# The triangular inverse of a recurrent scan: its loop rotated by half a pass on TensorE

## The reference, cut to what matters

```python
def step(s, inp):
    w, kk, a, k, v, r = inp
    sa = jnp.einsum('dbhij,dbhj->dbhi', s, kk)
    s = s * w[..., None, :] - sa[..., :, None] * (kk * a)[..., None, :] + v[..., :, None] * k[..., None, :]
    return s, jnp.einsum('dbhij,dbhj->dbhi', s, r)
return lax.scan(step, s0, scan_in)
```

## Time and profile before

| | us |
|---|---|
| median of 3 runs (lowest, highest) | 2728.82 (2727.08, 2732.63) |
| the profiled execution | 2732.08 |
| its span, first to last instruction | 2730.3 |
| PE busy in the span | 2520.4 (92%) |
| one pass of the inverse's loop | about 4.4 |
| the 8 steps of the scan | about 1511 to 1880 of the span |

### The profile page before, as it was taken

The page is one execution under the profiler, slowest core; times in us unless marked ns, Lnnn a source line. Parts: engine busy times, 40 slices in busy tenths (PEclk is TensorE's granted clock), DMA queues, the critical chain, the costliest instruction groups (busy, mean ns, idle before and its releaser), DMA issues.

```text
span 2730.3 us, 51612 instructions
## 1 busy us (share of the span) xinstructions
PE 2520.4 (92%) x22056; PEld 1724.2 (63%) x22056; DVE 1276.9 (47%) x2865; ACT 598.8 (22%) x1349; POOL 506.0 (19%) x418
## 2 busy tenths in 40 slices
PE   8999999999999999998999899999998977787887
PEld 6688785476886843444678888888866533333333
DVE  2873310037731101156448434444228667777765
ACT  1243000013330000115333444332002111111111
POOL 0000000000000000000012444430003455544452
PEclk9999999999999999999999999999999999888989
DMA  5333333344234435323352101003348999999997
GB/s 188 147 120 124 136 150 150 129 178 155 93 124 154 153 147 218 156 81 145 148 199 64 33 18 34 18 11 125 124 170 315 411 421 421 421 421 422 422 421 309
DMA packets 91234, 523.81 MB, mean 192 GB/s; under 512 B 39728, under 2 KB 39728, under 8 KB 43440
## 3 DMA queue, kind: packets, MB, share of 16 engines
q0 software_dynamic: 39360, 277.51, 24.9%
q1 hardware_dynamic: 51696, 243.80, 24.0%
HBM read 511.85 MB, written 9.44 MB: 191 GB/s over the span
## 4 chain that ended last, share of the span: by engine, by line
PE 68%; DVE 11%; DMA 10%; issue 3%; PEld 3%; ACT 2%; DVEq 2%; POOL 1%; ACTq 0%; PEldq 0%; SPq 0%; POOLq 0%
PE psum L523 34%; PE psum L1597 25%; DMA mem<-weights,mem 9%; DVE mem L2921 4%; PE psum L2052 4%; PEld psum L1597 3%; PE psum L765 2%; DVE mem L2428 1%; PE psum L539 1%; PE psum L2024 1%; POOL mem L3065 1%; DVEq L2549 1%; PE psum L1607 1%; DVE mem L2879 0%; DMA mem<-weights 0%
## 5 line engine op out<-in xcount | busy, mean ns | idle before, releaser
L1597 PE MATMUL psum<-mem 64*64 64x64 f32 (+5 forms) x16032 | 919.3, 258 | 51.2 <-issue 22.1
L523 PE MATMUL psum<-mem 128*128 128x256 f32 (+10 forms) x4248 | 954.9, 397 | 7.5 <-DVE mem L1079 3.3
L1597 PEld LDWEIGHTS psum<-mem 64*64 64x64 f32 (+2 forms) x16032 | 725.3, 144 | 244.5 <-issue 160.3
L523 PEld LDWEIGHTS psum<-mem 128*128 128x128 f32 (+5 forms) x4248 | 692.1, 182 | 262.6 <-issue 168.2
L2052 PE MATMUL psum<-mem 128*128 128x512 f32 x1024 | 501.5, 648 | 119.3 <-ACT mem L2392 119.3
L2052 PEld LDWEIGHTS psum<-mem 128*128 128x128 f32 x1024 | 207.5, 207 | 406.9 <-issue 244.4
L3065 POOL DMA_INDIRECT mem<-weights,mem x256 | 317.6, 1241 | 531.0 <-PE psum L2052 265.7
L2921 DVE CUSTOM_DVE_ANT_0 mem<-mem 128x1024 f32<-128x1024 f32 x256 | 307.4, 1224 | 140.0 <-DMA mem<-weights,mem 133.6
L2428 DVE TENSOR_TENSOR mem<-psum,mem 128x512 f32<-128x512 f32 (+1 forms) x193 | 131.1, 683 | 270.0 <-PE psum L1597 244.8
L2971 POOL TENSOR_TENSOR mem<-mem 128x512 f32<-128x512 f32 (+2 forms) x132 | 168.9, 1296 | 207.2 <-DVEq L2674 154.1
L2428 DVE TENSOR_TENSOR mem<-mem 128x512 f32<-128x512 f32 (+7 forms) x211 | 137.8, 661 | 89.2 <-ACTq L2160 67.5
(11 more groups left out here) (244 smaller groups left out, 1322.8 us busy)
## 6 DMA issues: line engine op xcount, KB each, us to landing
mem<-weights SPq DMA_DIRECT2D x100, 2048.0 KB, 7.3
rates_dram<-mem POOLq DMA_DIRECT2D x16, 512.0 KB, 4.9
mem<-rates_dram SPq DMA_DIRECT2D x32, 256.0 KB, 4.7
mem<-weights SPq DMA_DIRECT2D x7, 1024.0 KB, 6.0
mem<-weights SPq DMA_DIRECT2D x2, 2176.0 KB, 8.0
mem<-weights,mem POOLq DMA_INDIRECT x256, 26.4
mem<-weights SPq DMA_DIRECT2D x2, 1536.0 KB, 8.4
mem<-weights SPq DMA_DIRECT2D x2, 1152.0 KB, 8.8
```

The lines of the kernel that those rows point to most:

```text
L523: ins = pe.matmul(out, lhsT, rhs, start=start, stop=stop, skip_group_check=skip)
L1597: ins = pe.matmul(out, lhsT, rhs, start=start, stop=stop, skip_group_check=skip)
```

## The change

`inverse` is cut into `lefts(j)` and `updates(j)`. The left products of the first level in the loop are issued ahead of the opening of the four banks, the loop makes four passes of updates and then the next level's left products, and the last updates stand behind it. What is computed, and its order on PE, stays as it was.

```diff
         def inverse(h, left):
-            products = [[act_ring.open(pe, "held") for _ in range(2)] for _ in range(2)]
-            with pe.Fori(0, LEVELS - 1) as j:
+
+            def lefts(j):
                 for d in range(2):
                     pe.wait_ge(inverse_ready.sem, j * 2 + ((2 * LEVELS - 2) * h + d + 1))
...
                     last.then_inc(left_full.sem, 1)
+
+            def updates(j):
                 for d in range(2):
                     pe.wait_ge(left_ready.sem, j * 2 + ((2 * LEVELS - 2) * h + d + 1))
...
                     two.then_inc(inverseT_full.sem, 1)
+
+            lefts(0)
+            products = [[act_ring.open(pe, "held") for _ in range(2)] for _ in range(2)]
+            with pe.Fori(0, LEVELS - 2) as j:
+                updates(j)
+                lefts(j + 1)
+            updates(LEVELS - 2)
```

## The result

The changed kernel takes 2740.52 us (median of 12 runs, 2735.27 to 2746.24), the kernel before 2731.91 us beside it (12 runs, 2726.84 to 2737.07). The ratio is 1.0036, 95% interval 1.0027 to 1.0045: slower by 7.4 to 12.3 us, where I had forecast 3.1 us, "within". The profiled execution took 2739.89 us with a span of 2738.1, which is 7.8 us more than the span before.

The account below looks back on a forecast made before the run. PE was taken as the bound, with new code in steps 4 to 7 paced by its own loading. -4.4 - 0.4 + 0 + 5.3 + 2.6 = +3.1 us on 2728.8 gave 2731.9 us, range 2723 to 2739.

Parts of the forecast that it names:

- The opening: Ahead of the loop in steps 0 to 3: four PE waits for ACT's bank copies shrink to 0.15 us each, -4.4 us.
- The code: Doubled calls around the loop: 12 more instruction packets, +5.3 us in steps 4 to 7 and +2.6 in steps 0 to 3.
- Full pace: New code in steps 4 to 7 runs at its loading pace, 3.8 us a packet: +1.3 us per step, +5.3 taken.
- The first rival: Doubled code: packets come early enough, so the code term is 0; 2724.0 us, chance 0.18.
- The branch and the passes: At the loop: 40 branches back become 32, -0.4 us; moving the branch ahead of the updates changes remaining passes by 0.
- The sum: Whole kernel: the terms make +3.1 us on 2728.8, so 2731.9 us, "within".
- Code costs nothing: Doubled code: packets come early enough, leaving -4.8 us, so 2724.0 us; chance 0.18.
- Updates behind the loop run dry: Behind the loop: each of eight exits stalls 1.6 us for a packet, +12.8 us, so 2736.8 us; chance 0.16.
- Another collision: Packets against loads of the rates: one collision more 2737.4 us, chance 0.08; one less 2726.4 us, chance 0.05.
- The wait does not go: At the opening: the wait becomes one for direction 1's mask or `left_ready`, losing -4.4; 2736.3 us, chance 0.04.
- Shorter passes: In the loop: the branch is hidden wholly and ACT's chain moves up, -4.1 us more; 2727.8 us, chance 0.07.
- The signs I had named: In the scan: 138 packets, issue waits up 5 to 10 us, 0.5 to 1.5 us gaps behind exits, passes at 4.4 us.

Follow-up runs that it names:

- e7: e6 with the wait for the product banks moved into the loop, between left products and updates, as in e1; 2725.92 us, ratio 0.9970 to the kernel before.
- e2: The changed kernel with the product banks opened ahead of the first left products again; 2739.96 us, ratio 1.0028 to the kernel before.
- e13: The changed kernel again with one comment more and no instruction changed; 2739.47 us, ratio 1.0027 to the kernel before.
- e8: The changed kernel with the loads of the rates and step 7's weight load held back as in e6; 2728.29 us, ratio 0.9983 to before.
- e15: e8 with the product banks opened ahead of the first left products, leaving only the doubled code of the change; 2732.64 us, ratio 1.0003 to before.
- e1: The kernel before with the wait for the product banks moved into the loop, between left products and updates; 2738.66 us, ratio 1.0017 to before.
- e10: e7 with 128 semaphore increments on PE ahead of the scan, half an instruction packet; 2743.55 us, ratio 1.0042 to the kernel before.
- e3: The changed kernel with banks opened first, four passes in the old order and the fifth written behind the loop; 2743.48 us, ratio 1.0031 to before.
- e12: e6 with the first pass written out ahead of the loop, banks opened between its halves, four old-order passes in the loop; 2731.66 us, ratio 1.0002 to before.
- e5: The kernel before with one comment more and no instruction changed; 2731.95 us, ratio 0.9990 to the kernel before.
- e4: The changed kernel with banks opened first and all five passes written out, no loop; 2778.14 us, ratio 1.0160 to the kernel before.
- e6: The kernel before with SP's loads of the rates and step 7's weight load held back until PE's third loop pass; 2721.88 us, ratio 0.9955 to before.
- e14: The kernel before with only the loads of the rates held back until the third loop pass; 2726.30 us, ratio 0.9981 to before.
- e9: e6 with 128 semaphore increments on PE ahead of the scan, half an instruction packet; 2742.44 us, ratio 1.0037 to the kernel before.
- e11: e8 with 128 semaphore increments on PE ahead of the scan, half an instruction packet; 2756.49 us, ratio 1.0090 to the kernel before.

## Why the prediction was wrong

**The opening (-4.4 forecast, about -1.5 measured): this is the step that failed.** The mechanism was right as far as I looked. The four waits went, DVE's mask and ACT's banks were in time, PE went on after 0.15 us. Wrong was "so the four waits go and leave the ordinary 0.15 us each" as a gain of time. My own rows had the 1.60 and 1.69 us of "issue" 179 and 165 matmuls behind the very waits that I took away, and I had named packets as their cause; but I priced the two apart. They are two waits in series, of which the second ends at the arrival of a packet, and in steps 0 to 2 of e7 that didn't hang on the first. In the order of the changed kernel the gain was 1.6 us (after against e2; 0.9 us with e13's trace) and 1.5 us (e8 against e15). e1, e7 and e10 took the opening's wait away in the old order: 2.1, 1.2 and 2.1 us outside the repeated passes, which their own wait in the loop then made 1.8 to 3.2 us longer. Of 4.4 us never more than 2.1 came.

**The code (+7.9 forecast, 5 to 10 measured): right in kind, and in size only on the average.** e2's scan is 6.8 us longer, of which 1.9 us lie in its repeated passes (next paragraph), so 4.9 us; e3's is 9.8 us longer, all of it outside them. With the loads away e15 has 357.2 - 345.9 = 11.3 us with 3.2 in the repeated passes, so 8.1, and e12 10.2 with 0.4, so 9.8. "Full pace" in steps 4 to 7 was too simple, for the waits fall at the entry and in the first pass more than through straight code, and steps 0 to 3 had no more slack than the others. The first rival went by "mostly hidden" of the Trainium skill, Runtime: NRT & Kernel Launch, "Instruction fetch mechanics". It does not hold here: 12 packets more cost 0.4 to 0.8 us each, 48 more 0.97.

**The branch and the passes (-0.4 and 0 forecast, about +2 measured): the term that I put at nothing and that wasn't.** PE's sequencer at the loop's line, step 3, in the trace of before:

```profile
L1917 PEldq COMPARE_BRANCH  x5: 76/208/217, 1658.2 to 1676.0; - x5
```

and of after:

```profile
L1940 PEldq COMPARE_BRANCH  x4: 76/208/221, 1661.5 to 1675.5; - x4
```

Before, four passes took 17.8 us, 4.45 each; after, three took 14.0 us, 4.67 each. Over all eight steps the same reckoning gives 4.44 us (32 passes) and 4.54 us (24 passes): 24 x 0.10 = +2.4 us. Most steady passes take 4.43 to 4.49 us in both. It is the first repeated one that takes up to 4.87. The other kernels with 12 packets more tell whether the order or the code does this: in the changed order 24 passes average 4.53 us in e13 and 4.52 in e2, and in e3, with as much code in the old order, 4.44, of which this is step 3:

```profile
L1939 PEldq COMPARE_BRANCH  x4: 76/207/218, 1666.3 to 1679.7; - x4
```

With it go the waits for ACT's copy of `Dm`, 25 of them in e2 and 3 in e3. So the rotated body makes the passes longer, by 1.9 to 2.4 us in all, and the argument that DVE's mask covers the branch was not enough. What in the first repeated pass takes the time stays open.

**The sum.** -1.6 for the opening, +1.9 for the passes and +4.9 for the code make the +5.2 us in the scan of the changed kernel's first trace (+5.5 with e13 and e5). Against the terms of the forecast, the code is 3.0 us less and branch and passes are 2.3 us more: that these two cancel is luck, and what is left in the scan is the opening's missing 2.8 us. The runs say +8.6 by the medians. The 3 us between lie outside the scan in the traces: behind it 854.1 and 853.6 us before, 855.4 and 855.1 after, +1.4 us; the rest ahead of it, where no code changed and executions differ by as much. Whether the 1.4 us belong to the change is open: e3 and e12, with as many packets, have 854.3 and 853.6 us there.

**The rivals.** *Code costs nothing*: refuted by e2, e3 and e4. *Updates behind the loop run dry*, 2736.8 us, lay near the time (before's 2728.8 and the 8.6 measured are 2737.4) by a wrong mechanism, for no trace of the changed kernel has a gap at an exit, and e12, with nothing behind the loop, costs as much. *Another collision*, one more at 2737.4 us, hit the time by chance: the collisions moved as it said, but their number stayed, three waits of over 2 us before and after (step 4's is 2.20 us in place of 2.13). Step 5's 3.19 us became 1.89 and 1.17 us without a slow clock, and step 1 got one of 2.12 us. Windows of after, behind the gaps of steps 1 and 7 (stretch and its us, then busy us and count of PE, PEld, DVE, ACT, POOL, then PE's clock):

```profile
1570.00:1573.00 3.00, 3.00 (x74) 3.00 (x72) 1.38 (x2) 1.13 (x2) 2.86 (x4) 0.56 0.03 8
1853.00:1868.00 15.00, 11.89 (x381) 11.59 (x384) 5.99 (x9) 1.79 (x3) 0.00 (x0) 0.77 0.01 3
```

*The wait does not go*: it went, and most of its time stayed. The price I gave this case, 2736.3 us, was that of the true one; its mechanism (a wait for a mask) was not. *Shorter passes*: longer ones.

**The signs I had named.** 138 packets: right. Issue waits up by 5 to 10 us: 6.8 (10.1 in e13), right. New gaps of 0.5 to 1.5 us just behind the exits: wrong, they stand at the entries. Passes at 4.4 us: 4.54. A slow clock in another step than 4, 5 and 7, behind step 1's 2.12 us: it came. The chances were off more than the sum: a 7.9 us cost whose size I trusted, against a 4.4 us gain that rested on one unexamined "so it goes", was worth more than 0.28 for slower.

## What to carry to other kernels

Before a wait is priced as a gain, look for the next wait behind it on the same engine and ask whether its end depends on the first; if it ends with something that arrives at its own time (a packet of instructions, a transfer), only the part of the first that exceeds the second's slack is worth anything. And look at where the wait goes: put into a loop, it costs in every pass (0.1 us in each of 32 here, 3.1 us in e1, where it saved 2.1). Code written twice around a small loop costs by its packets, about 0.4 to 1 us per 256 instructions here, 4.9 to 9.8 us in all, so that doubling it to save 4.4 us was a loss even had they come whole. Where an engine fetches its code while it works, put bursts of data transfers into the loops in which it fetches none: two changed waits on SP, no work removed, brought 12 us (e6).

## What the runs showed of the hardware

- One semaphore increment on PE's sequencer took 0.156 us in a row of 128 of them (20.0 us idle), far more than the 0.05 us that such a record lasts in the trace.
- A single 2 MB load held back the instruction queue for 5.7 us, and the rates' bursts (4160 packets of some 250 B, six of them) cost 7.8 us in all (e14), though q8 needs 0.3% of the DMA engines' time.
- Half a packet's shift of all code of the scan moved the waits and left its time within 0.4 us in two pairs (e6 and e9, e8 and e11); in the third (e7 and e10) it took 2.6 us off.
- PE went on 1.2 to 1.6 us after the landing of a q8 packet at each of the 17 places in the changed kernel's scan where two matmuls start more than 0.8 us apart. A packet's transfer took 0.9 to 1.4 us in that scan.
- Behind the gaps of 2.12 and 3.24 us PE ran some us at 1.2 GHz (0.56 and 0.77 granted on average in the two windows of after above), but not behind the 2.20 us in step 4, nor anywhere in the scan of e13, whose longest wait was 2.41 us. With the loads away, e6 has no issue wait over 1.54 us in the scan and stayed at 2.4 GHz. So a late packet can cost more than its wait.
